# First block of a two-block transformer in one program: each sublayer's end and the next one's start done for x and then for the context, three weight columns side by side, and four shift tiles made by TensorE from conditions streamed as rows

## The chip, the cores and the metric

One core of a Trainium2 chip runs the whole program. The metric is the device time of one execution in microseconds (us), lower is better. The engines are PE (TensorE, with PEld for its weight loads), DVE (VectorE), ACT (ScalarE), and SP, whose queue issues the loads from memory. POOL does nothing here but four start-up memsets.

## The reference

Two blocks of depth 2 follow each other. The change is all in the first. Its state is `h` (x, 256 tokens) and `hc` (the context, 256 tokens), each of width 1024; every sublayer has the same frame for both, with modulation vectors that come from two conditions `c` and `c_ctx`:

```python
for i in range(DEPTH):                       # 2 layers, 3 sublayers each
    m  = adaln(c, ada_w[i], ada_b[i])        # silu(c) @ ada_w + b : shifts, scales, gates
    mc = adaln(c_ctx, ada_w[i], ada_b[i])
    h  = half_ffn(h, m, 0, ...)              # norm, scale/shift, w_in, silu gate, w_out, norm, gated add
    hc = half_ffn(hc, mc, 0, ...)
    u  = modulated_norm(h, g[2], m, 3)
    uc = modulated_norm(hc, g[2], mc, 3)
    y, yc = diff_attention_mixer(u, uc, ...)     # i == 0;  gqa_axial_mixer for i == 1
    h  = gated_residual(h, y, g[3], m, 3, 1.0)
    h  = half_ffn(h, m, 6, ...)
    if ctx_out:                                  # only i == 0
        hc = gated_residual(hc, yc, g[3], mc, 3, 1.0)
        hc = half_ffn(hc, mc, 6, ...)
```

A sublayer so ends with an RMS norm of its output and a gated add to `h`, and the next begins with an RMS norm of `h`, a scale and a shift. All products are done to about float32 accuracy.

## The kernel before

**Layout.** Activations lie with the 1024 features as 8 chunks of 128 partitions, and 512 tokens in the free dimension: 256 of x, then 256 of the context (`TT = 512`, `S = 256`). A product is made as three matmuls in a faster format (`three`, lines 432 to 434): high part of the weights by high and by low part of the input, low part of the weights by the high part. The weights come from memory in slots of 1 MB through a ring of 4 slots; a slot holds two halves (a half is one output column of 128 features, 8 chunks of it). For each half ACT makes the high part (`high`, line 1105, `w_hi`) and DVE the low part (`low`, line 1592, `w_lo`). There are NW = 3 buffers for halves, so the half for column n + 3 can be made only when PE is done with column n; PE signals that with `half_done`, ACT waits for it in `used()`, and PE waits for `w_lo` in `weights(h)`. Every engine runs its instructions strictly in the order written; semaphores order them against each other.

**Sublayers.** `sub` 0, 2, 3 and 5 are FFNs (FT = 22 column pairs into `ffn_in`, 22 halves out in `ffn_out`), 1 is the differential attention (DA), 4 the grouped attention (GA). The boundary between two sublayers is, for all 512 tokens at once:

1. the last products of the output: in an FFN the last three halves, chunk by chunk, 24 groups of three matmuls (the tail, `tail` in `ffn_out`); in DA eight columns (`project_out`);
2. ACT squares each chunk, DVE scales it out of PSUM, PE sums squares over the features with a matmul by ones (lines 486, 488 and 494);
3. ACT makes the inverse root (lines 1096 and 1097), DVE multiplies and adds to `hT` (`post`, lines 1632 and 1642), ACT squares the new `hT` (line 1119), PE sums (`norm_sum`, line 548), ACT makes the root;
4. DVE scales (line 1618), ACT adds the shift and rounds to `u_hi` (line 1138), DVE makes `u_lo` (line 1607), in pieces of 256 tokens: 16 pieces, chunk by chunk, x and context in turn;
5. PE does the first two weight columns side by side (`two_columns`), chunk by chunk as pieces come, and then a third whose weights are ready.

In DA the four value passes (`values`, 4 token tiles each) follow, then `scores(0)` and one whole column (`project(1, TT)`, the query of head 1), and then the 32 units of softmax. DVE's program there is `lows(2)`, two rotations, `lows(8)` (the low parts for the halves that follow the values), and then the maxima of unit 0. PE's `scores(1)` waits for `e_ready` 1, the exponentials of unit 0, and `turn(0)` for its probabilities.

**The start.** The modulation vectors of sublayer 0 are made first. A slot of kind "a" is multiplied on DVE (`ada_half`, line 1580, four passes a slot) by the conditions, which are loaded as a 1 MB tensor with the same row in all partitions (`condb`). A slot of kind "p" is multiplied on PE (`shifts`, line 538) by the conditions as columns. `FIRST` gives the order of the first 8 slots, `"apaapaaa"`. A slot is loaded again when the one 4 before it is consumed.

## Time and profile before

| | |
|---|---|
| time, median of 3 runs | 2549.24 us (2547.36 to 2554.26) |
| profiled execution: time, span | 2556.2 us, 2554.4 us |
| PE busy | 2434.4 us (95%) |
| PEld (weight loads) | 2063.6 us (81%) |
| DVE busy | 1598.0 us (63%) |
| ACT busy | 1056.0 us (41%) |
| DMA | 349.70 MB, mean 137 GB/s |
| chain that ended last | PE 89%, DVE 6%, ACT 3%, issue 1%, DMA 1% |
| granted TensorE clock, mean | 0.985 of full speed |

Busy time of PE is nearly the whole span, and the chain of work that ended last runs through PE for 89% of it. What is left is small: idle time of PE, and time in which PE is busy but at a lower clock.

### The profile page before, as it was taken

How to read it: one execution, taken by the hardware profiler on the slowest of the kernel's cores; microseconds unless marked ns; L12 is line 12 of the kernel's file. 1: busy time of each engine (PE TensorE's matmuls, PEld its weight loads, DVE VectorE, ACT ScalarE, POOL GpSimd, SP SyncE). 2: the span in 40 equal slices, each digit the busy share in tenths (PEclk: the TensorE clock that was granted, in tenths of full speed). 3: DMA queues.
4: the chain of work that ended last, by engine and by line, in shares of the span. 5: the costliest groups of instructions: out<-in, count | busy, mean ns of one | idle time of the engine just before them, and what ended most of it. 6: DMA issues, size and time to landing. Idle time of an engine off the chain costs nothing.

```text
span 2554.4 us, 34924 instructions
## 1 busy us (share of the span) xinstructions
PE 2434.4 (95%) x14062; PEld 2063.6 (81%) x14062; DVE 1598.0 (63%) x2791; ACT 1056.0 (41%) x1783; POOL 0.2 (0%) x4
## 2 busy tenths in 40 slices
PE   6999998999889999989999989899899999999998
PEld 4888886966658888868888858899898988999987
DVE  8777766366466666386623366555665866766757
ACT  3222324355542223242223245644545555455563
POOL 0000000000000000000000000000000000000000
PEclk9999999999989999999999999999999999999999
DMA  6555441211114554215422212255443533434422
GB/s 275 198 198 191 190 179 50 99 50 50 53 61 188 197 198 183 98 66 198 181 99 99 83 63 87 95 203 189 148 160 120 188 119 118 172 133 164 146 102 84
DMA packets 48832, 349.70 MB, mean 137 GB/s; under 512 B 5408, under 2 KB 5536, under 8 KB 6816
## 3 DMA queue, kind: packets, MB, share of 16 engines
q1 hardware_dynamic: 48672, 347.48, 36.6%
q8 instruction: 112, 1.84, 0.3%
q14 instruction: 48, 0.39, 0.0%
HBM read 346.41 MB, written 1.05 MB: 136 GB/s over the span
## 4 chain that ended last, share of the span: by engine, by line
PE 89%; DVE 6%; ACT 3%; issue 1%; DMA 1%; SPq 0%; DVEq 0%; ACTq 0%
PE ps L432 25%; PE ps L434 24%; PE ps L433 24%; PE ps L548 2%; DVE w_lo L1592 1%; PE ps L628 1%; PE ps L630 1%; PE ps L629 1%; PE ps L675 1%; PE ps L751 1%; ACT w_hi L1105 1%; PE ps L662 1%; DVE small L1761 1%; PE ps L777 1%; PE ps L851 1%
## 5 line engine op out<-in xcount | busy, mean ns | idle before, releaser
L1105 ACT ACTIVATE w_hi<-ring 128x1024 fp32r<-128x1024 f32 x504 | 533.5, 1060 | 1187.8 <-PE ps L434 1120.7
L1592 DVE TENSOR_TENSOR w_lo<-ring,w_hi 128x1024 fp32r<-128x1024 f32 x504 | 616.0, 1224 | 554.6 <-ACT w_hi L1105 551.6
L432 PE MATMUL ps<-u_hi,w_hi 128*128 128x512 f32 (+1 forms) x1744 | 639.2, 366 | 27.7 <-DVE u_lo L1607 26.2
L434 PE MATMUL ps<-u_hi,w_lo 128*128 128x512 f32 (+1 forms) x1744 | 635.7, 364 | 0.0
L433 PE MATMUL ps<-u_lo,w_hi 128*128 128x512 f32 (+1 forms) x1744 | 633.8, 363 | 0.0
L432 PEld LDWEIGHTS ps<-u_hi,w_hi 128*128 128x128 f32 x1744 | 330.4, 189 | 88.1 <-issue 33.4
L433 PEld LDWEIGHTS ps<-u_lo,w_hi 128*128 128x128 f32 x1744 | 330.4, 189 | 56.1 <-issue 1.0
L434 PEld LDWEIGHTS ps<-u_hi,w_lo 128*128 128x128 f32 x1744 | 330.5, 189 | 51.7
L1580 DVE CUSTOM_DVE_ANT_0 waste<-ring,condb,cols 128x1024 f32<-128x1024 f32 x280 | 346.5, 1279 | 8.3 <-DMA ring<-in_wk 8.3
L432 PE MATMUL ps<-uh,w_hi 128*128 128x256 f32 x1184 | 341.1, 288 | 10.2 <-DVE ul L1926 5.6
L433 PE MATMUL ps<-ul,w_hi 128*128 128x256 f32 x1184 | 330.2, 279 | 0.0
L434 PE MATMUL ps<-uh,w_lo 128*128 128x256 f32 x1184 | 330.2, 279 | 0.0
L434 PE MATMUL ps<-h_hi,w_lo 128*128 128x512 f32 (+1 forms) x704 | 257.9, 366 | 0.0
L432 PE MATMUL ps<-h_hi,w_hi 128*128 128x512 f32 (+1 forms) x704 | 257.3, 365 | 0.6 <-DVE h_lo L1664 0.5
L433 PE MATMUL ps<-h_lo,w_hi 128*128 128x512 f32 (+1 forms) x704 | 257.0, 365 | 0.0
L432 PEld LDWEIGHTS ps<-uh,w_hi 128*128 128x128 f32 x1184 | 223.8, 189 | 20.4 <-issue 16.3
L433 PEld LDWEIGHTS ps<-ul,w_hi 128*128 128x128 f32 x1184 | 223.8, 189 | 0.3
L434 PEld LDWEIGHTS ps<-uh,w_lo 128*128 128x128 f32 x1184 | 223.6, 189 | 0.0
L1678 DVE TENSOR_TENSOR hidden<-ps,hidden 128x512 f32<-128x512 f32 (+1 forms) x88 | 55.0, 625 | 204.2 <-PE ps L434 204.2
L432 PEld LDWEIGHTS ps<-h_hi,w_hi 128*128 128x128 f32 x704 | 132.3, 188 | 24.2 <-issue 1.1
L433 PEld LDWEIGHTS ps<-h_lo,w_hi 128*128 128x128 f32 x704 | 132.4, 188 | 24.0 <-issue 0.7
L434 PEld LDWEIGHTS ps<-h_hi,w_lo 128*128 128x128 f32 x704 | 132.5, 188 | 20.9
(302 smaller groups left out, 2642.4 us busy)
## 6 DMA issues: line engine op xcount, KB each, us to landing
ring<-in_wk SPq DMA_DIRECT2D x324, 1024.0 KB, 4.8
hT<-in_x SPq DMA_DIRECT2D x1, 2048.0 KB, 17.6
htabs<-in_htabs SPq DMA_DIRECT2D x1, 1152.0 KB, 7.1
condb<-in_crow SPq DMA_DIRECT2D x1, 1024.0 KB, 5.4
out_t<-uT SPq DMA_DIRECT2D x2, 512.0 KB, 2.6
trig<-in_trig SPq DMA_DIRECT2D x3, 256.0 KB, 5.3
wuk<-in_uk SPq DMA_DIRECT2D x2, 256.0 KB, 5.2
wuv<-in_uv SPq DMA_DIRECT2D x2, 256.0 KB, 6.0
```

Of the source, the lines that this page charges most:

```text
L432: mm(bank, hi, x_hi, start=first, stop=False)
L433: mm(bank, hi, x_lo, start=False, stop=False)
L434: return mm(bank, lo, x_hi, start=False, stop=last)
L548: last = mm(bankN[:, 0:T], tab("ones"), src[:, c * stride:c * stride + T], start=c == 0, stop=c == KC - 1)
L628: mm(bank, x_h, half_hi(h, n, n + 256), start=k == 0, stop=False)
L629: mm(bank, x_l, half_hi(h, n, n + 256), start=False, stop=False)
L630: last = mm(bank, x_h, half_lo(h, n, n + 256), start=False, stop=k == KC - 1)
L662: last = nc.tensor.transpose(ps[5 + u % 2][:, kt * P:(kt + 1) * P], specs[u]["prob"](u % 2, kt), tab("ident"))
L1105: f(half_hi(K, 0, HALF), ringed(n, K % 2 * HALF, (K % 2 + 1) * HALF), ACT.Copy).then_inc(whi_ready, 1)
L1580: last = nc.vector.tensor_tensor_reduce(waste[:, c * D:(c + 1) * D], ringed(slot, t * D, (t + 1) * D), condb[:, c * D:(c + 1) * D], 1.0, c ...
L1592: tt(half_lo(K, 0, HALF), ringed(HALF_SLOT[K], K % 2 * HALF, (K % 2 + 1) * HALF), half_hi(K, 0, HALF).bitcast(F32), ALU.subtract).then_inc ...
L1678: tt(h, bankV[v % 2][:, 0:T], h, ALU.mult).then_inc(v_free, 1)
```

## The change

It touches the first block alone, and of it the boundaries 0 to 1, 1 to 2, 2 to 3 and 3 to 4 (`PARTED`), the start, and the order of a few columns.

- FFN tail: the last three halves are multiplied for x alone (256 tokens), then for the context; with the context's groups come the sums of x's squares and, behind groups 19 to 23, the sums for x's next norm.
- DA output: columns 0 to 4 whole, the last three for x, then for the context; the same two sums are woven into the context's part.
- DVE and ACT do end and beginning for x (`post_part(sub, 0)`, `pre_part(sub + 1, 0)`), then for the context. Half of the context's output stays in PSUM until then.
- The next sublayer's first three weight columns go side by side (`first_columns`), first 8 chunks for x, the context's sums behind chunk 3, then 8 chunks for the context. In GA the third column is x's only.
- DA: the query column of head 1 is the third of these, so `project(1, TT)` is gone; `scores(0)` stands before the last value pass; the weights are packed in that order.
- Start: the conditions are one row of 8 KB; PE spreads it to all partitions with a matmul by ones, ACT takes it through SiLU into `condb`. `FIRST` is `"apapapap"`: 4 slots for DVE, 4 for PE. PE multiplies the "p" slots as the moving operand with the conditions stationary (`shift_rows`: 8 matmuls of 2 columns by 256), ACT copies the two rows, PE transposes them (`shift_columns`). Slots 2 and 3 of these come behind the first norm's sums.

```diff
-FIRST = "apaapaaa"
+FIRST = "apapapap"
+PARTED = (1, 2, 3, 4)
+X_SUM_AT = 2
+X_TERMS_AT = {19: (0, 2), 20: (2, 3), 21: (3, 4), 22: (4, 5), 23: (5, 8)}
+C_COPIED = 4
...
             sp.dma_start(cols[:, 0:NCOLS], cols_in).then_inc(cols_ready, 16)
-            sp.dma_start(condb[:, :], crow_in).then_inc(crow_ready, 16)
+            sp.dma_start(crow, crow_in).then_inc(crow_ready, 16)
...
+            def first_columns(pair, third, held, sums):
+                def block(bank, h, k, s):
+                    at_k = slice(k * TT + s * S, k * TT + (s + 1) * S)
+                    return three(bank[:, s * S:(s + 1) * S], half_hi(h, k * P, (k + 1) * P),
+                                 half_lo(h, k * P, (k + 1) * P), u_hi[:, at_k], u_lo[:, at_k], k == 0, k == KC - 1)
+                for s in range(2):
+                    if s:
+                        pe.wait_ge(rstd_ready, norms)
+                        for c in range(KC):
+                            pe.wait_ge(sq_ready, sq_seen + KC + c + 1)
+                            last = mm(bankN[:, S:TT], tab("ones"), sq[:, c * TT + S:(c + 1) * TT],
+                                      start=c == 0, stop=c == KC - 1)
+                        last.then_inc(ss_done, 1)
+                        norms += 1
+                    weights(H + 2)
+                    for k in range(KC):
+                        pe.wait_ge(ulo_ready, ulo_seen + s * KC + k + 1)
+                        for b in range(2):
+                            last = block(pair[b], H + b, k, s)
+                            if s and k == KC - 1:
+                                last.then_inc(half_done, 1)
+                        if not held:
+                            last = block(third, H + 2, k, s)
+                        elif k < KC - 1 if s == 0 else k == KC - 1:
+                            last = block(third, H + 2, k, 0)
+                        if s == 0 and k == 3:
+                            sums()
+                last.then_inc(half_done, 1)
...
+            def shift_rows(s):
+                for k in range(KC):
+                    last = mm(bankV[s % 2][0:2, 0:2 * P], cond[:, 2 * k:2 * k + 2],
+                              ringed(PE_SLOT[s], k * 2 * P, (k + 1) * 2 * P), start=k == 0, stop=k == KC - 1)
+                last.then_inc(row_done, 1)
...
             def ffn_out(T, sub):
...
+                    if (m, j) == (KC - 1, FT - NW) and parted:
+                        pe.wait_ge(y_copied, y_copies + 1)
+                        for jc in range(FT - NW, FT):
+                            last = chunk(jc, 0, S, TT)
+                        last.then_inc(y_done, 1)
+                    last = chunk(j, m, 0, S)
...
+                if parted:
+                    order = context_order(sub)
+                    for n in range(NW, NW * KC):
+                        j, i = FT - NW + (n - NW) // (KC - 1), (n - NW) % (KC - 1) + 1
+                        m = order[i]
+                        if j == FT - NW:
+                            pe.wait_ge(y_copied, y_copies + m + 1)
+                        last = chunk(j, m, S, TT)
+                        if i == KC - 1:
+                            last.then_inc(half_done, 1)
+                        elif j == FT - 1:
+                            last.then_inc(y_done, 1)
+                        if n == NW + X_SUM_AT:
+                            pe.wait_ge(yc_copied, yc_copies + 1)
+                            x_sums(ysq_ready, y_seen, 1)
+                        if n in X_TERMS_AT:
+                            x_terms(*X_TERMS_AT[n])
...
             def project_out(T, parted=False):
...
+                banks = [bank_a(), bank_a(), ps[2]]
+                a += 1
+                for s in range(2):
+                    for i in range(NW):
+                        weights(H + i)
...
+                            if s and n == X_SUM_AT:
+                                x_sums(yx_free, -ADDED)
+                            if s and n in X_TERMS_AT:
+                                x_terms(*X_TERMS_AT[n])
...
-                    scores(0)
-                    project(1, TT)
+                    for s in range(4):
+                        if s == 3:
+                            scores(0)
+                        values(4, after=turn_column if s == 0 else None, count=2)
```

On ScalarE:

```diff
+            def next_input(sub, behind, third_high):
+                third_high()
+                root(0)
+                for c in range(KC):
+                    piece_high(sub, c, 0)
+                    behind(c)
+                    if c == 5:
+                        root(1)
+                h_squares(1, 0, KC)
+                root(1)
+                for c in range(KC):
+                    piece_high(sub, c, 1)
+            def ffn_tail(sub):
+                for m in range(KC):
+                    if m == KC - 1:
+                        context(0)
+                    act.wait_ge(y_done, y_seen + m + 1 + (m == KC - 1))
+                    f(sq[:, m * TT:m * TT + S], ps[OUT_BANK[m]][:, 0:S], ACT.Square).then_inc(ysq_ready, 1)
+                root(0)
+                used()
+                h_squares(0, 0, 4)
+                used()
+                h_squares(0, 4, 6)
+                context(1)
+                h_squares(0, 6, 8)
+                context(2)
+                context(3)
+                next_input(sub + 1, behind, used)
```

On VectorE:

```diff
+            def next_input(sub, in_bank=()):
+                low()
+                pre_part(sub + 1, 0)
+                post_part(sub, 1, in_bank)
+                pre_part(sub + 1, 1)
...
-                    lows(2)
+                    lows(3)
                     dve.wait_ge(trig_ready, 16)
                     da_rope(0)
                     da_rope(1)
                     lows(8)
```

## Rows read from the trace of the kernel before

**Rows 1.** Waits of PE over the span: us in total, times, longest.

```profile
PE ps L432 <- DVE u_lo L1607: 26.2, 6, 6.9
PE ps L548 <- ACT sq L1119: 22.7, 6, 4.2
```

**Rows 2.** Timeline of PE, boundary 0 to 1: start, us, engine, line, operation [idle before].

```profile
413.11 1.98 PE L494 MATMUL ps<-sq,tabs 128*128 128x512 f32 x4
419.21 9.12 PE L548 MATMUL ps<-sq,tabs 128*128 128x512 f32 x16 [4.13 <-ACT sq L1119]
432.44 0.47 PE L432 MATMUL ps<-u_hi,w_hi 128*128 128x512 f32 x1 [4.11 <-DVE u_lo L1607]
...
446.31 0.35 PE L628 MATMUL ps<-w_hi,u_hi 128*128 128x256 f32 x1 [1.03 <-ACT qk L1271]
```

**Rows 3.** Window of boundary 0 to 1: length, PE busy, granted clock, DMA share, GB/s.

```profile
394.90:446.30 51.40, 42.09 (x145) 0.93 0.12 41
```

**Rows 4.** Timeline of DVE, boundary 0 to 1.

```profile
397.33 0.68 DVE L1664 TENSOR_TENSOR h_lo<-hidden,h_hi 128x512 fp32r<-128x512 f32 x1
...
429.83 1.28 DVE L1618 SCALAR_TENSOR_TENSOR uT<-hT,modA,rstd 128x256 f32<-128x256 f32 x3 [1.33 <-ACT rstd L1097]
...
441.31 1.28 DVE L1607 SCALAR_TENSOR_TENSOR u_lo<-uT,modt,u_hi 128x256 fp32r<-128x256 f32 x3
```

**Rows 5.** Timelines at boundary 5 to second block, 256 tokens: DVE, ACT, PE.

```profile
1837.15 0.75 DVE L1632 TENSOR_TENSOR yT<-yT,rstd 128x256 f32<-128x256 f32 x2
...
1835.81 0.47 ACT L1096 ACTIVATE rstd<-ps,cols 128x256 f32<-128x256 f32 x1
...
1832.49 0.59 PE L486 MATMUL ps<-sq,tabs 128*128 128x256 f32 x2
1832.92 0.59 PE L488 MATMUL ps<-sq,tabs 128*128 128x256 f32 x2
```

**Rows 6.** Windows of PE in dense columns, 512 wide and 256 wide.

```profile
200.00:210.00 10.00, 10.00 (x46) 1.00 0.47 170
1670.00:1680.00 10.00, 10.00 (x90) 1.00 0.51 174
```

**Rows 7.** Timelines where DA's softmax begins: DVE, ACT, PE.

```profile
490.77 2.58 DVE L1592 TENSOR_TENSOR w_lo<-ring,w_hi 128x1024 fp32r<-128x1024 f32 x2 [8.29 <-ACT w_hi L1105]
493.27 1.28 DVE L1761 TENSOR_REDUCE small<-ps 128x1 f32<-128x512 f32 x2
...
497.11 0.75 DVE L1780 SCALAR_TENSOR_TENSOR mix<-mix,small 128x512 f32<-128x512 f32 x1
...
495.46 0.68 ACT L1216 ACTIVATE mix<-ps,small 128x512 f32<-128x512 f32 x1
...
498.76 0.66 PE L761 MATMUL ps<-tabs,mix 128*128 128x128 f32 x4
```

**Rows 8.** Timelines of DA's output columns: ACT, then PE.

```profile
700.98 1.06 ACT L1105 ACTIVATE w_hi<-ring 128x1024 fp32r<-128x1024 f32 x1 [3.22 <-PE ps L434]
...
702.66 0.60 ACT L1201 ACTIVATE sq<-ps 128x512 f32<-128x512 f32 x1
...
716.02 1.13 PE L494 MATMUL ps<-sq,tabs 128*128 128x512 f32 x2 [1.50 <-ACT sq L1201]
```

**Rows 9.** Timeline of the start, all engines.

```profile
9.19 1.28 DVE L1580 CUSTOM_DVE_ANT_0 waste<-ring,condb,cols 128x1024 f32<-128x1024 f32 x1 [5.30 <-DMA ring<-in_wk]
...
21.89 4.27 ACT L1119 ACTIVATE sq<-hT 128x512 f32<-128x512 f32 x8 [13.30 <-DMA hT<-in_x]
...
24.39 6.99 PE L538 MATMUL ps<-cond,ring 128*128 128x2 f32 x32 [4.93 <-DMA ring<-in_wk]
...
31.24 8.51 PE L548 MATMUL ps<-sq,tabs 128*128 128x512 f32 x16
...
41.76 2.35 DVE L1592 TENSOR_TENSOR w_lo<-ring,w_hi 128x1024 fp32r<-128x1024 f32 x2
...
46.63 0.76 PE L432 MATMUL ps<-u_hi,w_hi 128*128 128x512 f32 x1 [6.88 <-DVE u_lo L1607]
```

More of the change, by code:

```diff
@@ L529, in two_columns, with x_sums @@
                 H += 2
-            def shifts(s):
-                pe.wait_ge(w_ready[PE_SLOT[s] % NRING], 16 * (PE_SLOT[s] // NRING + 1))
+            def x_sums(ready, seen, between=0):
+                nonlocal y_sums, norms
+                y_sums += 1
+                pe.wait_ge(rstd_ready, norms)
+                pe.wait_ge(ysum_ready, y_sums)
+                mm(bankN[:, 0:S], tab("ones"), sq[:, 0:S], start=True, stop=False)
+                for c in range(ADDED, KC):
+                    pe.wait_ge(ready, seen + c + 1 + (between if c == KC - 1 else 0))
+                    last = mm(bankN[:, 0:S], tab("ones"), sq[:, c * TT:c * TT + S], start=False, stop=c == KC - 1)
+                last.then_inc(ss_done, 1)
+                norms += 1
@@ new lines, in x_terms, with context_sums @@
+            def x_terms(c0, c1):
+                nonlocal norms
+                for c in range(c0, c1):
+                    if c == 0:
+                        pe.wait_ge(rstd_ready, norms)
+                    pe.wait_ge(sq_ready, sq_seen + c + 1)
+                    last = mm(bankN[:, 0:S], tab("ones"), sq[:, c * TT:c * TT + S], start=c == 0, stop=c == KC - 1)
+                    if c == KC - 1:
+                        last.then_inc(ss_done, 1)
+                        norms += 1
+            def context_sums(order, added, ready, seen):
+                nonlocal norms
+                pe.wait_ge(rstd_ready, norms)
+                pe.wait_ge(ysum_ready, y_sums)
+                c = order[0]
+                mm(bankN[:, S:TT], tab("ones"), sq[:, c * TT + S:(c + 1) * TT], start=True, stop=False)
+                for n in range(added, KC):
+                    c = order[n]
+                    pe.wait_ge(ready, seen + n + 1)
+                    last = mm(bankN[:, S:TT], tab("ones"), sq[:, c * TT + S:(c + 1) * TT],
+                              start=False, stop=n == KC - 1)
+                last.then_inc(ss_done, 1)
+                norms += 1
@@ L691, in softmax_units, with project_out @@
                 units += N
-            def project_out(T):
-                nonlocal o_seen
+            def project_out(T, parted=False):
+                nonlocal o_seen, a, H, out_first
                 o_seen += KC
-                first = a
-                for m in range(KC):
+                first = out_first = a
+                for m in range(ADDED if parted else KC):
                     weights(H)
@@ L735, in turn_column @@
                         rots += 1
-                    for s in range(4):
-                        values(4, after=turn_column if s == 0 else None, count=2)
                     def scores(u):
@@ L811, in _ @@
                     head_sum(DA_HEADS - 1)
[L812 removed]
+                    project_out(TT, True)
                 else:
@@ new lines, in h_squares, with y_part @@
+            def h_squares(s, c0, c1):
+                for c in range(c0, c1):
+                    act.wait_ge(h_ready, h_seen + s * KC + c + 1)
+                    n = c * TT + s * S
+                    f(sq[:, n:n + S], hT[:, n:n + S], ACT.Square).then_inc(sq_ready, 1)
+            def y_part(sub, m, s, bank):
+                k = sub * 16 + 2 * m + s
+                n = m * TT + s * S
+                return f(yT[:, n:n + S], bank[:, s * S:(s + 1) * S], ACT.Copy, scale=modC[:, k:k + 1])
@@ L1352, in _ @@
                     y_tiles(sub, S)
-                norm(S if sub >= 4 else TT)
+                if sub + 1 in PARTED:
+                    continue
+                norm(S)
                 if sub in FFN_SUBS:
@@ L1623, in pre, with pre_part @@
                 u_n += pieces
+            def pre_part(sub, s):
+                nonlocal norms, t_n, u_n
+                norms += 1
+                if s == 0:
+                    dve.wait_ge(mod_ready, sub + 1)
+                dve.wait_ge(rstd_ready, norms)
+                behind = 3
+                for j in range(KC + behind):
+                    if j >= behind:
+                        c = j - behind
+                        u_n += 1
+                        dve.wait_ge(u_ready, u_n)
+                        piece = slice(c * TT + s * S, c * TT + (s + 1) * S)
+                        shift = modt[:, sub * 48 + 2 * c + s:sub * 48 + 2 * c + s + 1]
+                        stt(u_lo[:, piece], uT[:, piece], shift, u_hi[:, piece].bitcast(F32),
+                            ALU.add, ALU.subtract).then_inc(ulo_ready, 1)
+                    if j < KC:
+                        n = j * TT + s * S
+                        k = sub * 16 + 2 * j + s
+                        stt(uT[:, n:n + S], hT[:, n:n + S], modA[:, k:k + 1], rstd[:, s * S:(s + 1) * S],
+                            ALU.mult, ALU.mult).then_inc(t_ready, 1)
+                        t_n += 1
```

362 lines of the change are left out of this document (279 added, 83 removed).

## The prediction

> **What bounds it now.** The table ahead says it first: PE is busy for 95% of the span and the chain that ended last runs through it for 89%. So only PE's idle time, and PE's time at a lower clock, can be won. I read the waits of PE next [rows 1]: 26.2 us in 6 waits for the low parts of a sublayer's input, 22.7 us in 6 for squares of the new state. The starts of the six sublayers and the second block's are where they lie. Then the timeline of one such boundary, 0 to 1 [rows 2]: PE ends the output's sums at 415.1, idles 4.1 us, sums the new norm from 419.2 to 428.3, idles 4.1 us again, does two columns from 432.4, and idles 1.0 us before the next product.
>
> How much is lost there? From the start of the tail to that product it is 51.4 us [rows 3]. The work in it: a 512-wide matmul starts every 0.228 us in dense columns (some 44 starts in 10 us, 46 rows with the two that reach in) and a 256-wide one every 0.114 us (88) [rows 6]. The tail is 72 matmuls, 16.4 us; two columns are 48, 10.9 us; a float32 sum costs 0.43 us at 256 tokens (1832.49 to 1832.92) [rows 5], so 0.86 at 512, 12 of them 10.3 us. That is 37.6 us, and 13.8 are lost: 9.3 in the three idles, 2.2 since the norm's eight sums come at DVE's pace (9.1 for 6.9 us), 1.8 since the two columns do too (DVE makes 16 pieces from 429.83 to 442.6, about 0.79 us each, 12.7 us for 10.9) [rows 2, 4], the rest clock.
>
> **The change at an FFN boundary (three of the four).** Splitting a matmul into two of 256 costs nothing by [rows 6]. The Trainium skill ("TensorE: Matmul & The Clock Gate", Back-to-back issue gap) gives each warm matmul a fixed 2.5 ns on top of its columns, which speaks against the split: an estimate from it is 144 more matmuls a boundary, 0.36 us, 1.4 us for four. The windows here show no such cost. The sums become 25 of 256, 10.75 us, 0.4 more. What PE loses after the change, step by step from the tail's start at 394.9:
>
> 1. The last half's low input is ready at 397.33 + 0.68 = 398.0 [rows 4]. Before, six chunks of 0.68 us (4.1) covered that; now six of 0.34 (2.05) reach 396.95. New idle: 1.1.
> 2. x's output sums, root and gated add (17 operations of DVE at 0.34, from 0.75 for two at 0.42 [rows 5]: 5.4 us) lie beside the context's 21 groups, 7.2 us. This is hidden. But the norm's sums end only with the last group, and then comes: `w_hi` for the third half, which now stands ahead of the root on ACT (about 1.0, from 1.06 [rows 8]), the root (Ln 0.47 [rows 5] and Exp alike, 0.9), one piece through DVE, ACT, DVE and PE (432.44 - 429.83 = 2.6 for two [rows 2, 4], less 0.8: 1.8), latencies. 3.8, against 4.1 now.
> 3. Behind chunk 3 the context's sums, and the root on ACT ahead of pieces 6 and 7: 0.3.
> 4. The context's gated adds come at 2 x 0.34 = 0.67 us a chunk, PE's sum takes 0.43: 7 x 0.24 = 1.7. Then root and first piece: 3.0. DVE gets to these adds only behind x's pieces, so x's three columns (8.2 us) don't cover them.
> 5. Three columns end together, so all three buffers come free together, at most 0.7 us apart. The next half needs `w_hi` 1.06 and `w_lo` 1.23 (2.35 for two [rows 9]): 2.0 of new idle. Before, the third column (5.5 us) ran meanwhile.
>
> With the 0.4 this is 12.3 us. Into DA (0 to 1) bank order makes step 5 2.6, so 12.9 against 13.8, a gain of 0.9. Into the FFN (2 to 3) there was no idle before the third column: 12.3 against 12.8, less the 0.5 of clock that both share, about 0. Into GA (3 to 4) x alone is in the third column, and the context's two columns go at DVE's pace again (0.8); it loses 0.6.
>
> **The clock.** After the idles before, the granted clock is 0.93 over the boundary [rows 3], 3.6 us at half speed in two stretches if the rest was full. Before, it cost only about 0.5, since sums and columns went at DVE's pace anyway. The Trainium skill (same page, Loop structure matters more than you think) says that waits between bursts of matmuls bring the array to its slow clock; the trace agrees. After the change, idles of 3.8 and 3.0 remain, and behind each stand three columns that PE itself bounds (1.03 us a piece against DVE's 0.79): a stretch at 1.2 GHz instead of 2.4 costs half its length, 1.7 us for one as long as the two here. I take 2.0 us more a boundary than before. Bounds: nothing, and 3.5.
>
> **Boundary 1 to 2.** Before: idles of 1.5 [rows 8], 4.2 and 4.1, sums at DVE's and the low clock's pace 3.0, columns 1.8: 14.6. After: both `bank_a()` calls stand ahead of the first matmul of the last three columns, and the second waits for the evacuation of column 4, which ends 703.26 - 700.98 = 2.3 us after its last matmul [rows 8]: 2.4. Steps 2 to 5: 3.7 + 0.2 + 1.7 + 3.0 + 2.0, and 0.4: 13.4. Gain 1.2.
>
> The four: 0.9 + 0 - 0.6 + 1.2 = +1.5; with 4 x 2.0 for the clock -6.5.
>
> **DA's start.** Now `w_lo` twice (490.77 to 493.35), maxima 1.28, exponentials to 496.14, probabilities to 497.86, `turn(0)` at 498.76 [rows 7]. `project(1, TT)`, 24 x 0.228 = 5.5 us, fills this. After the change the column is in front. `scores(0)` is earlier, but DVE's maxima are still behind `lows(8)`, whose last halves come free only with the last value product, at 490.9. PE's next instruction, `scores(1)`, waits for the exponentials: 490.9 to 496.3; `turn(0)` then at 498.0. That is 0.8 earlier with 5.6 less done: a loss of 4.8, and 5.4 us of idle before products that PE bounds: 1.2 for the clock. Loss 6.0. Queued behind on PE is the whole softmax; nothing else can go. Bounds: 4.1 (DVE's head start of one unit saves 0.7) and 7.5.
>
> **The start.** Now DVE's six slots run from 9.2 to 41.4, the norm's sums end at 39.8, two `w_lo` until 44.1, first product 46.6 [rows 9]. x is there at 21.9 and the next slot of 1 MB at 24.4, so a slot takes the DMA 2.5 us. With the 1 MB of conditions gone x comes at 19.4, and the fourth "a" slot, now seventh of the order, at 19.4 + 3 x 2.5 = 26.9; DVE's four passes take 4.9, so it ends near 31.8 and is no longer last. PE is. The new form costs it 8 sums of 256 a slot, 3.45 us at the high clock: two slots in front of the norm's sums, two behind, then a copy, two `w_hi` (2.0), one `w_lo` (1.2), the first two pieces (2.6). All at the high clock: x's first square at 20.1, + 6.9 + 6.9 + 0.5 + 2.0 + 1.2 + 2.6 = 40.2, a gain of 6.4. But the norm's sums take 8.5 now for 6.9 of work, though PE had been on the 32 small matmuls before them for 7 us [rows 9]: their first ones ran at the low clock. If all in front of the sums does too, spreading the conditions (4 x 1.7, from about 4.1) and two slots (6.9 each) end at 24.7, the sums at 33.2, two slots more at 40.1, and the first product comes at 46.4: no gain. I take 4, between the two.
>
> **Sum.** -6.5 - 6.0 + 4.0 = -8.5: the profiled execution's 2556.2 would become 2564.7. It is 7.0 above the median of the runs, 2549.2; nothing in the sum depends on that, so I give 2558 for the median.
>
> **Rivals.**
> - *Both signs cancel: no change (within 0.3%, 7.6 us, about what a measurement of this kernel can tell).* The clock stays high in the parted boundaries, since x's columns stand between two shorter idles, and the start gives 6: +1.5 - 5 + 6 = +2.5, 2547. For: idles of 1 and 2 us do nothing to the clock in the softmax stages. Against: 3.8 is nearly the 4.1 that always did. 0.30.
> - *Faster: x is through before the context's tail ends.* If the chain of step 2 ran beside the context's groups, as the code's two halves intend, both 4.1 us idles would go at four boundaries: 33 us, less 8 for step 5, 6 for DA, and 4 more from the start: 23 faster, 2526. It decides when x's norm sum ends 4 us before the last context group. Against: the last three terms are written behind group 23. For: DVE has 1.8 us to spare there. Half of that effect, 2538, counts here too. 0.16.
> - *Slower by more:* each idle of step 2 and 4 is followed by a long stretch at 1.2 GHz (3.5 a boundary), and the start gives nothing: +1.5 - 14 - 7 = -19.5, 2569. 0.14.
> - The forecast, 2553 to 2564: 0.40.
>
> The forecast's own range, 4 to 15 slower, has 0.11 of its 0.40 within 7.6; of the first rival 0.05 falls beyond it on the slow side and 0.01 on the fast one. Slower 0.29 + 0.05 + 0.14 = 0.48, same 0.11 + 0.24 = 0.35, faster 0.17. The range holds the forecast, the first rival and most of the third: 2541 to 2569.
>
> **What would show it.** In PE's waits `u_lo` near 36 us in 10 times (4 x 3.8, 4 x 3.0, and the two other starts) and the squares of the new state far below 22.7; an idle of about 5 us on PE before `scores(1)`; 2 us before the fourth column of each sublayer; the granted clock at half behind x's and the context's first piece; first product near 42. It is wrong if the PE idle before x's first product is below 2 us, or if DVE reaches the maxima before the last values are done.

## The result and the profile after

| | kernel before | changed kernel |
|---|---|---|
| median of 7 runs each | 2549.99 us | 2567.75 us |
| lowest, highest | 2547.36, 2554.57 | 2560.91, 2574.04 |
| profiled execution, its span | 2556.2, 2554.4 | 2560.91, 2559.1 |
| PE busy in the span | 95% | 96% |

The ratio is 1.0060, 95% interval 1.0046 to 1.0074: 15.3 us slower (11.7 to 18.9), where 2558 was forecast for the median. In a second series the same kernel gave 1.0052 (1.0036 to 1.0069), 13.3 us. The two profiled executions are only 4.7 us apart, since before's was a long one of its kernel and after's the shortest of its own; the last section shows one reason why executions of one kernel differ that much.

The waits of PE after (line of the waiting matmul, releaser, us in total, times, longest), which answer to [rows 1]:

```profile
PE ps L458 <- DVE u_lo L1958: 24.5, 8, 3.5
PE ps L458 <- DVE u_lo L1926: 8.4, 2, 5.5
PE ps L943 <- ACT mix L1515: 7.6, 3, 5.3
PE ps L659 <- ACT sq L1315: 7.3, 3, 3.4
PE ps L458 <- DVE h_lo L2066: 3.6, 4, 1.1
PE ps L458 <- DVE w_lo L1911: 3.5, 2, 1.7
PE ps L458 <- ACT sq L1478: 2.4, 1, 2.4
```

Input low parts and squares of the new state took 48.9 us in [rows 1]. Now the same two take 24.5 + 8.4 + 7.3 = 40.2, and the four others, which the change made or made longer, 17.1 in all (before had 2.8 of these: 2.3 for `mix`, 0.5 for `h_lo`). The idle of the boundaries was not removed, it changed place. Over the whole span PE's idle did fall, from 120.0 us to 114.1, because the start's waits for loads shrank from 16.9 us to 4.3. PE's busy time rose by 10.6, from 2434.4 to 2445.0 (to 2450.3, with 114.7 idle, in the second trace of the same kernel, number 12). So in the profiles the loss is busy time: products at the lower clock, and products that start further apart. The timeline of PE at boundary 0 to 1, for [rows 2], shows each place: before the tail's last half, before x's first product, before the context's, and before the next half's product.

```profile
393.69 0.35 PE L458 MATMUL ps<-h_hi,w_hi 128*128 128x256 f32 x1 [1.06 <-DVE h_lo L2066]
416.87 0.36 PE L458 MATMUL ps<-u_hi,w_hi 128*128 128x256 f32 x1 [3.24 <-DVE u_lo L1958]
...
429.13 5.08 PE L613 MATMUL ps<-sq,tabs 128*128 128x256 f32 x16
437.02 0.36 PE L458 MATMUL ps<-u_hi,w_hi 128*128 128x256 f32 x1 [2.81 <-DVE u_lo L1958]
...
449.67 0.36 PE L781 MATMUL ps<-w_hi,u_hi 128*128 128x256 f32 x1 [2.45 <-ACT qk L1582]
```

1.06, 3.24, 2.81 and 2.45: the forecast's steps had 1.1, 3.8, 3.0 and 2.6. Why x's chain isn't through earlier is seen on ACT and DVE:

```profile
412.38 1.08 ACT L1301 ACTIVATE w_hi<-ring 128x1024 fp32r<-128x1024 f32 x1
413.67 0.47 ACT L1292 ACTIVATE rstd<-ps,cols 128x256 f32<-128x256 f32 x1 [0.21 <-PE ps L577]
414.17 0.42 ACT L1293 ACTIVATE rstd<-rstd 128x256 f32<-128x256 f32 x1
```

```profile
413.92 1.22 DVE L1911 TENSOR_TENSOR w_lo<-ring,w_hi 128x1024 fp32r<-128x1024 f32 x1
415.06 1.27 DVE L1963 SCALAR_TENSOR_TENSOR uT<-hT,modA,rstd 128x256 f32<-128x256 f32 x3
416.24 0.48 DVE L1958 SCALAR_TENSOR_TENSOR u_lo<-uT,modt,u_hi 128x256 fp32r<-128x256 f32 x1
```

The third half's conversion on ACT and its low part on DVE, 1.1 and 1.2 us, stand around the root, and x's first low part comes at 416.24, when PE has nothing left.

The attention's begin, PE and what it waits for, for [rows 7]:

```profile
496.58 0.28 PE L783 MATMUL ps<-w_lo,u_hi 128*128 128x256 f32 x1
502.14 2.08 PE L943 MATMUL ps<-qk 64*128 64x512 f32 x4 [5.29 <-ACT mix L1515]
504.15 1.12 PE L953 MATMUL ps<-tabs,mix 128*128 128x128 f32 x4
```

```profile
496.62 2.58 DVE L1911 TENSOR_TENSOR w_lo<-ring,w_hi 128x1024 fp32r<-128x1024 f32 x2 [9.57 <-ACT w_hi L1301]
499.12 1.28 DVE L2166 TENSOR_REDUCE small<-ps 128x1 f32<-128x512 f32 x2
```

The scores of unit 0 have long been in their bank, but the maxima (L2166) stand on DVE behind two low parts whose halves come free only with the last value products. And the start, PE, for [rows 9]:

```profile
11.46 8.98 PE L641 MATMUL ps<-ring,cond 128*2 128x256 f32 x32 [0.62 <-DMA ring<-in_wk]
...
22.38 7.13 PE L659 MATMUL ps<-sq,tabs 128*128 128x512 f32 x16 [1.19 <-ACT sq L1315]
29.45 7.07 PE L641 MATMUL ps<-ring,cond 128*2 128x256 f32 x32
...
42.79 0.77 PE L458 MATMUL ps<-u_hi,w_hi 128*128 128x512 f32 x1 [5.53 <-DVE u_lo L1926]
```

The first product comes at 42.8 instead of 46.6. The first two slots' rows take 8.98 us, partly at the low clock, the next two 7.07: between the two ends that the forecast had.

The windows of PE (length, busy and count, granted clock, DMA share, GB/s) at the attention's begin and in the whole of boundary 0 to 1 and the begin:

```profile
500.00:504.00 4.00, 1.86 (x4) 0.50 0.72 262
504.00:508.00 4.00, 4.00 (x16) 0.66 0.02 4
...
384.80:600.10 215.30, 196.50 (x1228) 0.97 0.17 62
```

### The profile page after: what moved, and what is told of

Same layout as the page of the kernel before. It is cut to its first block, busy times and chain, and to the rows that moved or that the text cites. A ratio compares the mean times of both kernels' runs of the same rounds, so it can differ in the third digit from the quotient of the medians.

```text
span 2559.1 us, 36408 instructions
## 1 busy us (share of the span) xinstructions
PE 2445.0 (96%) x14732; PEld 2107.5 (82%) x14732; DVE 1584.3 (62%) x2825; ACT 1068.9 (42%) x1877; POOL 0.2 (0%) x4
## 4 chain that ended last, share of the span: by engine, by line
PE 88%; DVE 7%; ACT 3%; issue 1%; DMA 1%; SPq 0%; DVEq 0%; ACTq 0%
PE ps L458 25%; PE ps L459 24%; PE ps L460 24%; DVE w_lo L1911 2%; PE ps L781 1%; PE ps L782 1%; PE ps L783 1%; ACT w_hi L1301 1%; PE ps L828 1%; PE ps L943 1%; PE ps L613 1%; PE ps L659 1%; DMA hT<-in_x 1%; PE ps L815 1%; DVE small L2166 1%
## 5 line engine op out<-in xcount | busy, mean ns | idle before, releaser
L458 PE MATMUL ps<-u_hi,w_hi 128*128 128x512 f32 (+1 forms) x1856 | 662.4, 357 | 39.6 <-DVE u_lo L1958 24.5
L459 PE MATMUL ps<-u_lo,w_hi 128*128 128x512 f32 (+1 forms) x1856 | 655.6, 353 | 0.0
L460 PE MATMUL ps<-u_hi,w_lo 128*128 128x512 f32 (+1 forms) x1856 | 651.7, 351 | 0.0
L458 PEld LDWEIGHTS ps<-u_hi,w_hi 128*128 128x128 f32 x1856 | 354.9, 191 | 94.4 <-issue 38.4
L459 PEld LDWEIGHTS ps<-u_lo,w_hi 128*128 128x128 f32 x1856 | 355.6, 192 | 46.0 <-issue 0.5
L460 PEld LDWEIGHTS ps<-u_hi,w_lo 128*128 128x128 f32 x1856 | 354.4, 191 | 46.9
L458 PE MATMUL ps<-h_hi,w_hi 128*128 128x512 f32 (+1 forms) x776 | 270.9, 349 | 3.6 <-DVE h_lo L2066 3.6
L458 PEld LDWEIGHTS ps<-h_hi,w_hi 128*128 128x128 f32 x776 | 145.7, 188 | 24.9 <-DVE w_lo L1911 4.3
L459 PEld LDWEIGHTS ps<-h_lo,w_hi 128*128 128x128 f32 x776 | 145.8, 188 | 18.5
L460 PEld LDWEIGHTS ps<-h_hi,w_lo 128*128 128x128 f32 x776 | 145.8, 188 | 18.4
```

Source lines behind the costliest of these rows:

```text
L458: mm(bank, hi, x_hi, start=first, stop=False, skip_group_check=skip)
L459: mm(bank, hi, x_lo, start=False, stop=False, skip_group_check=skip)
L460: return mm(bank, lo, x_hi, start=False, stop=last, skip_group_check=skip)
```

## The experiments

All times by ratio are the ratio's distance from 1 times 2551, the median of before on that chip (2550.9 to 2551.7 in the three series); intervals are 95%. They reach 3.3 to 4.8 us to each side, so a difference between two kernels that are both measured against before is uncertain by about 5 us, an estimate from the two intervals. Smaller differences below are not shown by the times alone.

**1. The start alone, with work left out (e_start).** The list of parted boundaries is emptied, and the first attention's front and the bank order are put back. This kernel leaves out part of the computation: in the three whole tails of FFNs the last three halves are multiplied for x alone, 24 chunks, 8.2 us of matmuls in each, 24.6 in all.

```diff
-PARTED = (1, 2, 3, 4)
+PARTED = ()
```

> The kernel before with the new start alone: conditions as one row, FIRST in turns, shift rows as moving operand; no boundary is parted, and DA and GA begin as before. Theory (the start is worth what the two traces show, its first product comes about 5.0 us earlier and nothing gives that back): 5 us faster than before, 2545, ratio 0.998, and the w_hi of every later column 5.0 us earlier than before. Rival A (the start is where the changed kernel's medians lose what its profile does not show, 9 us beyond the 8 of its trace): 2553 or more. Rival B (hidden later, since the first FFN waits for slots of the ring): within 1 us of before, and the 5 us are gone after the first FFN.

Measured: 2539.87 us median, ratio 0.9950 (0.9931 to 0.9968), 12.8 us below before. With 24.6 us of work left out that says little about the start: the trace shows new waits of PE in those tails (`PE ps L512 <- DVE sq L2050: 7.1, 3, 2.4` among them), so the work left out was not all won. Number 5 is the same with whole tails.

**2. The attention's begin (e_early).** The changed kernel, with maxima, probabilities and exponentials of unit 0 ahead of the last value pass: on DVE two of the eight low parts, on ACT the fourth value pass, are moved behind them.

```diff
-                    lows(8)
+                    lows(6)
...
                     probabilities(u)
+                    if held and u == 0:
+                        held()
```

> The changed kernel with one thing moved: in DA, VectorE does unit 0's maxima and probabilities ahead of the low parts that wait for the last value pass, and ScalarE the exponentials of unit 0 ahead of that pass' tiles. Theory (the 5.3 us of idle before scores(1) come of the maxima standing behind lows(8), and the clock falls behind it): that idle is gone, 5 to 6 us faster than the changed kernel, about 2562. Rival (the softmax stages are bound by VectorE's chain, so the idle only moves to a later unit): the idle before scores(1) is gone, but idle of the same size stands before the turns of units 1 to 3, and the time stays at 2567.

Measured: 2556.21 us, ratio 1.0020 (1.0006 to 1.0033): 5.1 us above before, and 8 to 10 below the changed kernel, where 5 to 6 was expected. The 5.3 us wait before `scores(1)` is gone. First the waits at `scores` over the span, then in this attention alone (480 to 620); the 1.8 stands in a later sublayer and stood there before too:

```profile
PE ps L943 <- ACT mix L1515: 2.8, 3, 1.8
```

```profile
PE ps L943 <- ACT mix L1515: 0.5, 1, 0.5
```

The waits at the turns (L953) grow only from 10.1 to 11.1 us, so the rival by which the idle just moves there falls.

```profile
391.10:597.80 206.70, 191.86 (x1227) 0.99 0.18 64
```

The stretch that took 215.3 us after takes 206.7, 8.6 less: 4.0 of idle (18.8 against 14.8) and 4.6 of busy time; the granted clock rises from 0.97 to 0.99. Not all of the 4.6 belongs to the begin: in the changed kernel's trace the clock is at half for 6.8 us at the begin and for two stretches of 3.4 in the boundary before it, in number 2's for one stretch of 3.4 in the boundary and not at all at the begin.

**3. The split alone (e_split).** The kernel before, with each column that is made by itself (135 of them; the two side by side and the FFN's outputs stay as they are) done as eight chunks of x and then eight of the context; no order between engines is changed.

```diff
-                for k in range(KC):
+                for c0 in range(0, T, S):
+                    for k in range(KC):
...
-                    at_k = slice(k * stride, k * stride + T)
+                        at_k = slice(k * stride + c0, k * stride + c0 + S)
```

> The kernel before with every whole column of 512 tokens made as 8 chunks for x and then 8 for the context, in one PSUM bank, nothing else moved: 135 columns, 3240 matmuls more (FFN columns after the first pair, DA's query column and its output columns). It measures by itself what halving the width costs. Prediction's term (nothing, 0.114 against 0.228): 2550. The two spacings that the traces after show for 256 wide matmuls, 113 and 118 ns against 228 for 512: 0 us if all are at 113, 24 us slower if all are at 118 (2574). Apart from these: the fixed 2.5 ns a matmul of the Trainium skill (TensorE: Matmul & The Clock Gate, Back-to-back issue gap), an estimate from that page, would make it 8 us slower, 2558.

Measured: 2563.31 us, ratio 1.0053 (1.0035 to 1.0071): 13.5 us slower. The page counts 17302 matmuls for before's 14062, so 3240 were split, at 4.2 ns each on average (2.8 to 5.6), between the ends that were expected, nothing and 24 us. Windows of this kernel in its first, second and third FFN, all in dense 256-wide columns at the full clock:

```profile
200.00:210.00 10.00, 10.00 (x88) 1.00 0.57 211
...
900.00:910.00 10.00, 10.00 (x91) 1.00 0.54 211
1250.00:1260.00 10.00, 10.00 (x88) 1.00 0.46 167
```

The same instruction starts 91 or 88 times in 10 us (a few of them reach in from before). Between starts it is 0.113 or 0.118 us; two of the first are 0.227, two of the second 0.235, one of 512 wide is 0.229 in most stretches. [Rows 6] had caught only a stretch of 0.113. So the 4.2 ns is a mean over two cases: against 0.229, a split costs about 6 ns where the halves go at 0.118, as in the first and third FFN here, and wins about 2 where they go at 0.113, as in the second.

**4. Boundary 2 to 3 whole, with work left out (e_no3).** The changed kernel with 3 taken from the list. Here too the whole tail leaves out the context's part of the last three halves, 8.2 us of matmuls.

> The changed kernel with boundary 2 to 3 (FFN to FFN) made whole again as before; the other three stay parted. Theory (by the traces this boundary loses about 2.1 us by the parting: new idle before the last half and before the fourth column, against the two idles of 4.1): 2 us faster than the changed kernel, 2566, the two idles of 4.1 us back, none of 1.0 and 2.0. Rival (parting an FFN boundary gains by itself, and the loss is all in DA): 2 to 4 us slower than the changed kernel.

Measured: 2557.92 us, ratio 1.0026 (1.0013 to 1.0039), 8.7 us below the changed kernel. That is about the work left out, so nothing follows; number 8 is the same without the gap.

**5. The start alone (e_start2).** As number 1, but the whole tails multiply all of `T`:

```diff
-                    last = chunk(j, m, 0, S)
+                    last = chunk(j, m, 0, S if parted else T)
```

> The kernel before with the new start alone (rows of the first shift parted past the conditions, the second's in the norm's wait), all four boundaries and the differential attention's begin as before. Nothing is left out. Theory of the steps: 5.0 us below the kernel before (4.5 to 5.5), as the two profiles' first w_hi of the first sublayer stand to each other. Rival: the run of the start that left out products worth 24.6 us of TensorE and gained only 12.7 us by its ratio; if that ratio may be read so, the start alone gains nothing and this kernel is up to 12 us above the kernel before.

Measured: 2546.59 us, ratio 0.9987 (0.9973 to 1.0001): 3.3 us below before (6.9 below to 0.3 above), where 5.0 was expected. The first product comes at 43.05 in its trace, 3.6 us earlier than before's 46.63, and the low part of the 61st half, near the first FFN's end, still 3.2 earlier (365.5 for 368.7): nothing gives the gain back. The time fits this, and the reading of number 1 by which the start would cost up to 12 us falls; that it gains nothing the time alone just doesn't exclude.

**6. Boundary 0 to 1 with the begin (e_one).** The start, `PARTED = (1,)`.

> The new start and, of the four boundaries, 0 to 1 alone, with the new begin of the differential attention. Nothing is left out. Theory of the steps (profile): start -5.0, boundary 0 to 1 and the attention's begin together +10.1, so 5.1 us above the kernel before. Rival, my prediction's terms: gain 0.9 of the boundary less 6.0 of the begin and clock +2.0 saved, hence 4 to 1 us below it. Rival of the spacing: the parted sections also set the next stretches to the longer spacing of the matmuls (0.1177 for 0.1133 us at 256 columns), then up to 7 us more for each sublayer that it reaches: 8 to 15 above.

Measured: 2554.55 us, ratio 1.0024 (1.0009 to 1.0040): 6.1 us above before, 9.4 above number 5. The same stretch of work, first in number 5 and then here:

```profile
386.40:592.40 206.00, 192.12 (x1058) 0.98 0.18 64
```

```profile
383.30:599.00 215.70, 196.85 (x1227) 0.97 0.17 62
```

9.7 us longer: idle 18.9 for 13.9, busy 196.9 for 192.1. The profile and the series of runs agree, and the steps' 5.1 above before is near the 6.1. The expectation's rival is not what the prediction says: it takes the clock's 2.0 as saved, while the prediction adds it as lost. With the right sign the prediction's terms are -4.0 + 7.1, 3.1 above before, which the interval (2.3 to 10.2) holds too.

**7. Boundary 1 to 2 alone (e_two).** The start, `PARTED = (2,)`, and the three banks of the parted output columns taken one at a time, so that the first column doesn't wait for column 4's evacuation.

```diff
-                banks = [bank_a(), bank_a(), ps[2]]
-                a += 1
+                banks = []
...
+                        else:
+                            banks.append(bank_a() if i < 2 else ps[2])
```

> The new start and, of the four boundaries, 1 to 2 alone, with its banks taken one at a time instead of all three ahead. Nothing is left out. Theory of the steps: start -5.0, boundary -1.2 (profile), the wait for the bank -2.4: 8.6 us below the kernel before. Rival: the sections of 256 columns cost 1 to 2 us by their spacing and the bank's wait turns into one for the next tile: 5 us below. Rival of the spacing that outlasts its section: 0 to 2 us above.

Measured: 2546.45 us, ratio 0.9977 (0.9962 to 0.9992): 5.9 us below before, the fastest whole kernel of the study. Against number 5 it is 2.6 us lower, which the two intervals don't separate from nothing; 8.6 below before was expected, and 5 by the rival. The wait for the square at the bank is gone; the only wait of its kind left is the 1.4 us at the output's sums that before had too (1.50 in [rows 8]):

```profile
PE ps L520 <- ACT sq L1484: 1.4, 1, 1.4
```

**8. Boundary 2 to 3 whole (e_no3b)** and **9. boundary 3 to 4 whole (e_no4)**, each with the rest of the changed kernel and nothing left out: `PARTED = (1, 2, 4)` and `(1, 2, 3)`.

> The changed kernel with boundary 2 to 3 whole again, as in the kernel before; boundaries 0 to 1, 1 to 2 and 3 to 4, the attention's begin and the start as changed. Nothing is left out. Theory of the steps: 2.1 us below the changed kernel (profile: boundary 2 to 3 lost 2.1), ratio to the kernel before 1.005. Prediction: boundary 2 to 3 costs 0 but for the clock's 2.0 saved, so 2 us above the changed kernel, ratio 1.007. Rival of the spacing: 5 to 9 us below the changed kernel, ratio 1.003 to 1.004, since one source of the longer spacing is gone.

> The changed kernel with boundary 3 to 4 whole again, as in the kernel before. Nothing is left out. Theory of additive parts (start -3.3, 0 to 1 with the begin +9.4, 1 to 2 +2.6, 2 to 3 +4.6, sum 13.3, and the whole change +15.3): 2 to 5 us below the changed kernel, ratio 1.0045 to 1.0055. Theory of the profiles alone (3 to 4 lost 2.0): 2 us below. Prediction: boundary 3 to 4 gains 2.0 from the clock and loses 0.6, so this kernel would be 1.4 us above the changed one, ratio 1.0065.

Measured: number 8 gave 2562.14 us, ratio 1.0042 (1.0027 to 1.0057), number 9 gave 2559.64 us, ratio 1.0038 (1.0021 to 1.0056). Against the changed kernel's two ratios, 1.0060 and 1.0052, parting boundary 2 to 3 would cost 2.6 to 4.6 us and parting boundary 3 to 4 3.6 to 5.6; each is within what two such ratios leave uncertain. Both expectations again take the clock's 2.0 as saved by the parting. The prediction has it as lost, so by its terms number 8 should be 2.0 and number 9 2.6 below the changed kernel. The steps' theory gives nearly the same, and the runs don't tell these apart, nor the rival of the spacing for number 8 (5 to 9 below). Windows of boundary 2 to 3, whole in number 8, with the stretches at the low clock:

```profile
1074.90:1185.60 110.70, 102.42 (x410) 0.97 0.29 109
1116.10:1119.50 3.40, 3.40 (x6) 0.51 0.00 0
1129.80:1133.20 3.40, 3.40 (x10) 0.50 0.00 0
```

and parted in the changed kernel:

```profile
1070.10:1183.80 113.70, 104.86 (x580) 0.97 0.29 107
1114.00:1117.40 3.40, 3.40 (x19) 0.55 0.01 2
1134.40:1137.80 3.40, 3.40 (x20) 0.56 0.00 0
```

3.0 us longer. The idle is nearly the same, 8.8 for 8.3, and the clock is at half for as long in both. It is the busy time that grows, 104.9 for 102.4. Whole, the first low stretch falls on 6 records of float32 sums, which come at DVE's pace, and the second on 10 of the 512-wide products of the two columns side by side, which take 12.7 us in all: just what DVE needs for its 16 pieces. So neither stretch costs much. Parted, both fall on 256-wide products that PE itself bounds, 19 and 20 of them, and cost up to half their length, 3.4 us in all. The 170 matmuls more, 144 of them from splits, add the rest.

**10. Boundaries 0 to 1 and 1 to 2 with both repairs (e_12).** The start, `PARTED = (1, 2)`, the early maxima of number 2 and the banks of number 7.

> The new start, boundaries 0 to 1 and 1 to 2 parted, the attention's first maxima, probabilities and exponentials ahead of the last value pass, and boundary 1 to 2's banks taken one at a time; boundaries 2 to 3 and 3 to 4 whole. Nothing is left out. Theory A, that the attention's begin carries nearly all of the +9.4 measured for boundary 0 to 1 and that begin together: the boundary itself costs 0 to 1 us, so with the start and the 2 us of the bank this kernel is 5 to 6 us below the kernel before, like the kernel with 1 to 2 alone. Theory B, that the parted boundary itself costs what 2 to 3 costs (4.6 us): 1 to 2 us below the kernel before.

Measured: 2548.93 us, ratio 0.9993 (0.9980 to 1.0006): 1.8 us below before, 4.1 above number 7. By the medians theory B, that the boundary itself costs something like the others; but the intervals reach to both, and this kernel's trace has the stretch at 206.9 us (206.0 in number 5, 206.7 in number 2), which is theory A. The same stretch here, in number 11 (both repairs too) and in number 12 (no repair):

```profile
384.90:591.80 206.90, 192.07 (x1228) 0.99 0.18 65
```

```profile
383.60:593.30 209.70, 194.87 (x1228) 0.98 0.18 64
```

```profile
386.40:603.40 217.00, 198.26 (x1228) 0.96 0.17 62
```

In the traces of number 2 and number 10 the clock falls once in the boundary, for 3.4 us. In the six other traces with this boundary parted and nothing left out it falls twice in it or just behind it, for 6.8 us in all or, in number 12, for 10.2. PE's idles there are the same in all eight, 3.2, 2.8 and 2.5 us, so their length alone doesn't decide it. Boundary 0 to 1 by itself then costs about 1 us when the clock falls once (206.9 for 206.0) and about 4 when it falls twice (209.7, one trace), the more frequent case.

**11. The changed kernel with both repairs (e_bank)** and **12. the changed kernel again (again).**

> The changed kernel with two repairs: the attention's first maxima, probabilities and exponentials ahead of the last value pass (as in the run before, which came 10 us below the changed kernel), and boundary 1 to 2's three banks taken one at a time (the 2.4 us wait for the square). Nothing is left out. Additive theory: 12 to 13 us below the changed kernel, ratio 1.001. Rival, that the bank's wait only moves to the next tile: 10 us below, ratio 1.002.

> The changed kernel itself once more, beside the others on this chip. If the additive theory holds, its ratio is that of the first measurement, 1.006, and that of the sum of the parts; if the first measurement was high by chance, 1.004, and the parts sum to less.

Measured: number 11 gave 2559.27 us, ratio 1.0026 (1.0012 to 1.0040), number 12 gave 2562.58 us, ratio 1.0052 (1.0036 to 1.0069). Against the two ratios of the changed kernel the repairs win 6.6 to 8.7 us, not 12 to 13. Number 11 is not better than number 2, which has the begin's repair alone, though the 2.4 us wait is gone from its trace. The bank's repair is worth less than these runs can tell.

**The parts by all traces.** The twelve kept traces in which nothing is left out give each part once more. DVE makes 504 low parts in every kernel; the time from the start of one to the start of another is the length of the same piece of work. Each length, in us, is the median, with the lowest and highest:

| low parts | contains | whole | parted |
|---|---|---|---|
| 65 to 89 | boundary 0 to 1 and the begin | 206.1 (205.7 to 206.8) | 216.2 (214.4 to 217.4), with early maxima 207.3 (207.1 to 210.1) |
| 89 to 119 | boundary 1 to 2 | 241.3 (240.5 to 243.6) | 244.4 (240.4 to 246.3) |
| 164 to 183 | boundary 2 to 3 | 130.7 (129.1 to 131.4) | 132.3 (130.7 to 132.4) |
| 229 to 244 | boundary 3 to 4 | 100.3 (100.2 to 101.3) | 102.6 (101.8 to 104.5) |

The differences are 10.1, 3.1, 1.6 and 2.3 us; the first and the last are clear of the spread, the middle two are not. The first product comes at 42.4 (41.0 to 43.2) with the new start, 4.3 us earlier than before's 46.6. Together this is 12.8 us slower, near the 13.3 and 15.3 of the times. The lengths still hold the chance of each trace, of the clock and of the spacing that the last section describes. It also shows no gain from boundary 1 to 2: number 7, the fastest kernel, has 240.4 there and number 5, with this boundary whole, 240.5.

## Why the prediction was right, and where its sizes were off

The direction was right, and so was the mechanism: idle moved rather than removed, the attention's begin laid bare, part of it given back by the start. The size was 8.5 us for a measured 13.3 and 15.3. The first series' median, 2567.75, lies outside the forecast's own 2553 to 2564. It is inside the wide range, which held no change at all too, only because the range reaches to the rival that is slower still; and that rival let the start give nothing, where it gave about 4. The second series' 2562.58 is inside both. Term by term (a loss is positive):

| term | predicted | by ratios | by windows or timelines | by all traces |
|---|---|---|---|---|
| start | -4.0 | -3.3 | first product -3.8 | -4.3 |
| boundary 0 to 1 with the begin | -0.9 + 2.0 + 6.0 = 7.1 | 9.4 | 9.7 | 10.1 |
| of it, the begin | 6.0 | 8 to 10 | at most 8.6 | 6.1 to 9.1 |
| boundary 1 to 2 | -1.2 + 2.0 = 0.8 | -2.6 with the banks' repair | not separated | 3.1, not separated |
| boundary 2 to 3 | 0 + 2.0 = 2.0 | 2.6 to 4.6, not separated | 3.0 | 1.6, not separated |
| boundary 3 to 4 | 0.6 + 2.0 = 2.6 | 3.6 to 5.6, not separated | not measured | 2.3 |

- **Idles at a boundary.** The steps were a little too long: 1.1 for 1.06, 3.8 for 3.24, 3.0 for 2.81, 2.6 for 2.45, 10.5 for 9.6 in all. The sum has one slip: the 0.5 us of clock that before pays is taken off at 2 to 3 and not at 0 to 1. x's root did come late, behind the third half's `w_hi`, as step 2 said, and the rival by which x is through ahead of the context's tail falls: it needed 4 us, and the wait stayed at 3.24.
- **"Splitting a matmul into two of 256 costs nothing by [rows 6]"** is the term that was wrong. Number 3 measures 4.2 ns a split. The changed kernel has 670 matmuls more (14732 for 14062), of which 552 come from splits of products (the rest are sums and the start's), which makes 2.3 us, with number 3's interval 1.5 to 3.1. Two windows of 10 us at different places could not show it: each spacing has two values, and the 256-wide window happened to lie in a short one. The Trainium skill ("TensorE: Matmul & The Clock Gate", Back-to-back issue gap), weighed there with 2.5 ns a matmul, had the sign right; the runs give more, 4.2 on average, and the traces no fixed cost but the two cases of number 3.
- **The attention's begin** was 4.8 us of idle and 1.2 of clock. The wait came as said, behind `lows(8)` (5.29 for 5.4), and the idle of the whole stretch fell by 4.0 when it was cured. The clock's part was too small: the granted clock is at half for 6.8 us, of which PE is busy for 4.6 (502.1 to 506.7), up to 2.3 us lost for the 1.2. The two errors nearly cancel. Like with like, two low stretches in the boundary before, the begin costs 6.1 (216.2 less number 11's 210.1); against the two traces with one stretch it seems to cost 9, but some 3 us of that are the boundary's.
- **The clock at the boundaries**, 2.0 each, was too small as well: at 2 to 3 the low stretches are as long as before, but lie on products that PE bounds and cost up to 3.4 us where before, by the forecast's own working, paid about 0.5: up to 2.9 more for the 2.0. At 0 to 1 the boundary by itself costs about 4 with two stretches, for a forecast of 1.1.
- **The start** is right to within a microsecond.
- **1 to 2.** The wait of 2.4 us for the bank was there to the tenth. A gain of 1.2 less 2.0 for the clock was forecast; the traces have the stretch 3.1 us longer, within their spread.

By all traces, then, the miss lies in boundary 0 to 1 with the begin (3.0 us) and perhaps in 1 to 2 (2.3). That it comes of the low clock on dense products and of the splits is what the two bullets on them make likely; the terms are not separated that far. Boundaries 2 to 3 and 3 to 4 came out near the forecast as sums, at 2 to 3 with idles too long and clock and splits too small, which is luck. Of the signs that the forecast named, the low parts' waits are 32.9 us in 10 times (36 said), the wait before `scores(1)` 5.3 (5) and the first product 42.8 (42). The profiled pair alone would have hidden this: 4.7 us, less than the forecast.

## What to carry to other kernels

Before work is put side by side to cover a wait, ask which engine is asked for the next operand when it all ends at once, and what stands behind the instruction that was moved on each of the other queues: here a column of 5.5 us had been the cover of maxima and exponentials two engines away, and moving it cost more than the start's shortening gained. A low clock costs by what it falls on: where another engine sets the pace behind the wait it was nearly free here, on dense matmuls behind the same wait it cost up to half its length. And the best kernel of the study, 5.9 us below before, keeps the new start and one parted boundary whose tail is columns, but by its trace it owes nothing to that boundary. Parting an FFN's tail was not seen to pay at any of the three: by the traces the stretches came out longer, at 2 to 3 within the spread.

## What the runs showed of the hardware

Dense matmuls have two spacings at a granted clock of 1.00, which last for tens to hundreds of microseconds and change between executions of the same instructions. Windows of 200 us with 512-wide columns, before in its third FFN and in its first (behind length comes busy time and count of PE, PEld, DVE, ACT and POOL, then granted clock, DMA share, GB/s):

```profile
1160.00:1360.00 200.00, 200.00 (x859) 162.01 (x858) 99.55 (x128) 48.26 (x57) 0.00 (x0) 1.00 0.40 153
100.00:300.00 200.00, 200.00 (x876) 164.09 (x875) 141.90 (x200) 49.79 (x59) 0.00 (x0) 1.00 0.50 194
```

and the same stretch of the same code, the first FFN, in the changed kernel and in number 2:

```profile
100.00:300.00 200.00, 200.00 (x875) 164.14 (x874) 145.09 (x207) 50.86 (x60) 0.00 (x0) 1.00 0.49 189
```

```profile
100.00:300.00 200.00, 200.00 (x859) 162.00 (x858) 142.28 (x199) 49.88 (x58) 0.00 (x0) 1.00 0.50 189
```

0.229 or 0.233 us a matmul, 2% of the time: a whole FFN in the longer spacing takes some 6 us more, an estimate from 4.4 ns on its some 1450 dense products. That is as much as the effects under study, and a part of the spread of one kernel's runs (before: 2541 to 2566 us in 92 of the three series' 93). 256-wide matmuls show the same, in windows of PE from 1665 to 1775, in before and then in the changed kernel:

```profile
1665.00:1775.00 110.00, 109.93 (x968) 1.00 0.53 192
```

```profile
1665.00:1775.00 110.00, 110.00 (x936) 1.00 0.53 191
```

And one and the same kernel shows both: the last value products of the first attention, in the changed kernel's first trace and in its second.

```profile
487.00:495.00 8.00, 8.00 (x73) 1.00 0.35 131
```

```profile
490.00:498.00 8.00, 8.00 (x70) 1.00 0.40 131
```

What sets the value is open. The DMA's share alone doesn't: it is 0.50 and 0.49 in windows of 0.229 and 0.50 in one of 0.233. The width alone doesn't either, since number 3 has both. With two values whose choice these kernels don't set as far as is known, one profiled pair can't rank kernels half a per cent apart; twelve runs against some thirty of before could here only to about 3.5 us.
